# Splitting streamed fp32 weights in place, two chunks ahead, in a two-block transformer kernel

## What is computed

```python
h = x                                                   # first block, 256 tokens
u = rmsnorm(h, g_mix)
qa, ka, va, qb, kb, vb = split(u @ w_in, 6)
h = h + concat(rmsnorm(dilated(qa, ka, va)), rmsnorm(moba(qb, kb, vb))) @ w_out
h = h + memory_cross_attention(rmsnorm(h, g_cross), rmsnorm(mem, g_mem), ...)
h = h + conv_ffn(rmsnorm(h, g_ffn), w_gate, w_up, conv_w, conv_b, w_down)
xl, xc = rmsnorm(h, g_final), ctx                       # second block, 256 + 256 tokens
for l in range(2):
    sh1, sc1, g1, ... = split(silu(c) @ ada_w[l] + ada_b[l], 9)      # the same for c_ctx
    xl = post_norm(xl, 0.5 * g1 * swiglu(modulate(xl, sh1, sc1), ffn1_w_in[l], ffn1_w_out[l]))
    # xc in the same way; then the mixer, the even one (gated linear attention and latent
    # attention) for l = 0, the odd one (neighbourhood attention) for l = 1:
    xl = post_norm(xl, g2 * mixer(modulate(xl, sh2, sc2), modulate(xc, ...)))
    xl = post_norm(xl, 0.5 * g3 * swiglu(modulate(xl, sh3, sc3), ffn2_w_in[l], ffn2_w_out[l]))
    # xc too, but not after the last mixer
```

## Time and profile before

| | |
|---|---|
| median of 3 runs | 2248.92 us (2247.44 to 2249.53) |
| the profiled execution | 2245.71 us, of which its span 2243.9 us |
| granted TensorE clock | 0.998 of full speed |
| PE busy | 2195.9 us, 98% of the span, 13158 matmuls |
| DVE, ACT, POOL busy | 1392.7, 937.4 and 685.3 us |
| DMA | 329.94 MB, 147 GB/s on average |

### The profile page before, as it was taken

The page is one execution under the profiler, slowest core; times in us unless marked ns, Lnnn a source line. Parts: engine busy times, 40 slices in busy tenths (PEclk is TensorE's granted clock), DMA queues, the critical chain, the costliest instruction groups (busy, mean ns, idle before and its releaser), DMA issues. The chain is left out here.

```text
span 2243.9 us, 33497 instructions
## 1 busy us (share of the span) xinstructions
PE 2195.9 (98%) x13158; PEld 1893.8 (84%) x13158; DVE 1392.7 (62%) x2125; ACT 937.4 (42%) x1552; POOL 685.3 (31%) x321
## 2 busy tenths in 40 slices
PE   8999999999999999989999999999999999989999
PEld 8988899998888877757788888788888878879998
DVE  4655454478878577675776675687655484347335
ACT  5664455542222255354522223342222254465443
POOL 3433345422222233221122222412222243213444
PEclk9999999999999999999999999999999999999999
DMA  8446545554554322111244533334544262214553
GB/s 304 153 187 244 188 161 196 174 198 175 191 225 163 107 96 78 66 39 38 104 161 147 189 142 120 106 140 170 196 174 162 88 156 88 76 39 167 169 194 110
DMA packets 79579, 329.94 MB, mean 147 GB/s; under 512 B 19088, under 2 KB 29456, under 8 KB 55872
## 3 DMA queue, kind: packets, MB, share of 16 engines
q1 hardware_dynamic: 79424, 327.81, 41.2%
HBM read 326.70 MB, written 1.08 MB: 146 GB/s over the span
## 5 line engine op out<-in xcount | busy, mean ns | idle before, releaser
L2280 POOL TENSOR_TENSOR WL<-WF,WH 128x1024 fp32r<-128x1024 f32 (+1 forms) x244 | 580.8, 2381 | 1347.8 <-ACT WH L1098 1347.4
L554 PE MATMUL ps<-Hh,WH 128*128 128x256 f32 (+1 forms) x2288 | 593.1, 338 | 3.5 <-ACT Hh L1227 1.5
L558 PE MATMUL ps<-Hh,WL 128*128 128x256 f32 (+1 forms) x2288 | 589.5, 337 | 2.6 <-DVE WL L1624 2.1
L562 PE MATMUL ps<-Hl,WH 128*128 128x256 f32 (+1 forms) x2288 | 588.9, 336 | 0.8 <-DVE Hl L1634 0.8
L1098 ACT CAST WH<-WF 128x1024 fp32r<-128x1024 f32 (+2 forms) x501 | 460.9, 957 | 283.7 <-PE ps L562 265.0
L554 PEld LDWEIGHTS ps<-Hh,WH 128*128 128x128 f32 x2288 | 393.8, 190 | 54.9 <-issue 8.0
L558 PEld LDWEIGHTS ps<-Hh,WL 128*128 128x128 f32 x2288 | 394.8, 190 | 49.3 <-DVE WL L1624 3.8
L562 PEld LDWEIGHTS ps<-Hl,WH 128*128 128x128 f32 x2288 | 395.0, 190 | 46.1 <-DVE Hl L1634 1.0
L1702 DVE CUSTOM_DVE_ANT_0 TMP<-AR 128x1024 f32<-128x1024 f32 x216 | 394.9, 1868 | 17.8 <-DMA AR<-in_ada 16.9
L1624 DVE TENSOR_TENSOR WL<-WF,WH 128x1024 fp32r<-128x1024 f32 (+2 forms) x263 | 313.8, 1194 | 101.7 <-ACT WH L1098 101.1
L558 PE MATMUL ps<-HIDh,WL 128*128 128x512 f32 (+1 forms) x880 | 305.4, 347 | 1.6 <-DVE WL L1624 1.6
(11 more groups left out here) (264 smaller groups left out, 2241.2 us busy)
## 6 DMA issues: line engine op xcount, KB each, us to landing
WF<-in_w SPq DMA_DIRECT2D x170, 1024.0 KB, 4.8
AR<-in_ada SPq DMA_DIRECT2D x120, 512.0 KB, 5.7
WF<-in_w SPq DMA_DIRECT2D x80, 704.0 KB, 4.1
AR<-in_piece SPq DMA_DIRECT2D x12, 1024.0 KB, 7.7
AR<-bias_rows SPq DMA_DIRECT2D x12, 256.0 KB, 7.1
AR<-in_rpb SPq DMA_DIRECT2D x12, 256.0 KB, 6.4
AR<-in_cond SPq DMA_DIRECT2D x2, 1024.0 KB, 7.4
X<-in_x SPq DMA_DIRECT2D x2, 512.0 KB, 4.1
```

The source lines that it names most:

```text
L554: e.matmul(b, h[:, k, col], hi[:, 0:T], start=x == 0, stop=False)
L558: e.matmul(b, l[:, k, col], hi[:, 0:T], start=False, stop=False)
L562: m = e.matmul(b, h[:, k, col], lo[:, 0:T], start=False, stop=x == n - 1)
L2280: e.tensor_tensor(l[:, k0:k1, :], src[:, k0:k1, :], h[:, k0:k1, :].bitcast(F32), ALU.subtract).then_inc(*up("p_lo", ("lo", i, q)))
```

## The change

The staged chunk and the low part now share memory: four buffers, each seen as `WF[i]` (fp32) and as `WL[i]` (F32R), so that DVE and POOL write the low part over the chunk they read. The high part has three buffers. The number of bytes is the same (seven chunks' worth). Chunk i+2 is split at position i everywhere, into slots that chunk i-3 of its own number frees. The hand-written splits in the seams are gone, POOL casts no weights any more except half 1 of chunk 0, and `eout` and `nout` split at all four c. In `pool_mixer_out` the additions of squares at c == 2 now come ahead of the splits. SP waits for the end of chunk i-4 before it loads chunk i, and the modulation step is called for chunk i-2 instead of i-3. Cut to its core:

```diff
-    WF = [sb(f"WF{i}", SLOT)[:, :] for i in range(3)]
-    WH = [None, None]
-    WL = [None, None]
-    for i in range(2):
-        WH[i], WL[i] = sb(f"WH{i}", SLOT, F32R)[:, :], sb(f"WL{i}", SLOT, F32R)[:, :]
+    WF, WL = [], []
+    for i in range(4):
+        with nc.sbuf_tensor(f"WL{i}", [P, SLOT], F32R) as low:
+            pass
+        WL.append(low[:, :])
+        WF.append(sb(f"WF{i}", SLOT)[:, :])
+    WH = [sb(f"WH{i}", SLOT, F32R)[:, :] for i in range(3)]
...
-        return WF[i % 3][:, 0:n].rearrange("p (k c) -> p k c", k=nk(i))
+        return WF[i % 4][:, 0:n].rearrange("p (k c) -> p k c", k=nk(i))
 
     def parts_of(i):
-        n, s = chunk_floats(PLAN[i]), TURN[i] % 2
-        return (WH[s][:, 0:n].rearrange("p (k c) -> p k c", k=nk(i)),
-                WL[s][:, 0:n].rearrange("p (k c) -> p k c", k=nk(i)))
+        n = chunk_floats(PLAN[i])
+        return (WH[i % 3][:, 0:n].rearrange("p (k c) -> p k c", k=nk(i)),
+                WL[i % 4][:, 0:n].rearrange("p (k c) -> p k c", k=nk(i)))
...
-        n = TURN[i]
-        if n + 1 < len(WIDE) and WIDE[n + 1] in SECOND or i in SECOND:
-            return [WIDE[n + 2]]
-        return [WIDE[n + 1]] if n + 1 < len(WIDE) and not (n and WIDE[n - 1] in SECOND) else []
-
-
-
-    SECOND = {CH[name][j] for name, j in (("f0_gu", 1), ("f10_gu", 1), ("e_lr", 0), ("f20_gu", 1),
...
+        return [i + 2] if i + 2 < len(PLAN) else []
+
+    LAST = "f21"
...
-        n = TURN[i]
-        if n < 2:
+        if i < 3:
             return None
-        old = WIDE[n - 2]
+        old = i - 3
...
-        act_half(e, CH["f10_gu"][1], 0)
         act_root(e, "final", S, D, 0)
-        act_half(e, CH["f10_gu"][1], 1)
...
-        i = AFTER[st]
-        if i:
-            act_half(e, i, 0)
...
-            if c < 3:
-                act_splits(e, CH["eout"][c])
+            act_splits(e, CH["eout"][c])
             if c == 2:
-                act_half(e, CH["f20_gu"][0], 0)
                 for k in range(4):
                     act_collect(e, "mix0", k, T2)
-                act_half(e, CH["f20_gu"][0], 1)
...
+        act_split(e, 1)
...
-                if j == 7:
-                    act_half(e, CH["qm"][0], 0)
                 act_square(e, HT[j], X[:, j, lat], ("wsq", j), ("wx", j))
-        act_half(e, CH["qm"][0], 1)
...
+        act_splits(e, CH["vm"][3])
...
-            if k == 3:
-                dve_split(e, AFTER[before], 1)
...
-        if AFTER[st]:
-            dve_split(e, AFTER[st])
...
-        last, [then] = CH[name][3], splits_at(CH[name][3])
         for c in range(4):
-            if c < 2:
-                dve_splits(e, CH[name][c])
-            if c in (1, 2):
-                dve_split(e, last, c - 1)
+            dve_splits(e, CH[name][c])
...
-                if j == 7:
-                    for q in range(2 if T == T2 else 1):
-                        dve_split(e, then, 1 - q)
...
-    def pool_round(e, i):
-
-        src, (h, _) = staged(i), parts_of(i)
-        k0, k1 = halves(i)[1]
-        e.wait_ge(*at(("wf", i)))
-        if slot_freed(i, 1):
-            e.wait_ge(*at(slot_freed(i, 1)))
-        e.tensor_scalar(h[:, k0:k1, :], src[:, k0:k1, :], 1.0, None, ALU.mult).then_inc(*up("p_hi", ("hi", i, 1)))
-
-    def pool_end_norm(e, st):
-        if AFTER[st]:
-            pool_round(e, AFTER[st])
...
-        pool_end_norm(e, st)
...
-        for c in range(3):
-            if c < 2:
-                pool_splits(e, CH[name][c])
+        for c in range(4):
             if c == 2:
-                if T < T2:
-                    pool_split(e, splits_at(CH[name][3])[0], 0)
                 for k in (1, 2, 3):
                     pool_collect(e, st, k, T)
-        pool_end_norm(e, st)
+            pool_splits(e, CH[name][c])
...
-        if i >= 3:
-            old = i - 3
-            for q in range(len(halves(old))):
-                e.wait_ge(*at(("hi", old, q)))
-                e.wait_ge(*at(("lo", old, q)))
+        if i >= 4:
+            e.wait_ge(*at(("end", i - 4)))
         src = bass.AP(a_w.tensor, int(starts[i]), [[n, P], [1, n]])
-        e.dma_start(WF[i % 3][:, 0:n], src).then_inc(*dma(f"wf{i % 3}", ("wf", i)))
+        e.dma_start(WF[i % 4][:, 0:n], src).then_inc(*dma(f"wf{i % 4}", ("wf", i)))
...
-            if i - 3 in MOD_STEP:
-                sp_mod_step(e, *MOD_STEP[i - 3])
+            if i - 2 in MOD_STEP:
+                sp_mod_step(e, *MOD_STEP[i - 2])
```

More of the change, by code:

```diff
@@ L355, in program @@
         CH.setdefault(c[0], []).append(i)
-    WIDE = list(range(len(PLAN)))
-    TURN = {i: n for n, i in enumerate(WIDE)}
     def nk(i):
@@ L367, in staged @@
         n = chunk_floats(PLAN[i])
-        return WF[i % 3][:, 0:n].rearrange("p (k c) -> p k c", k=nk(i))
+        return WF[i % 4][:, 0:n].rearrange("p (k c) -> p k c", k=nk(i))
     def parts_of(i):
-        n, s = chunk_floats(PLAN[i]), TURN[i] % 2
-        return (WH[s][:, 0:n].rearrange("p (k c) -> p k c", k=nk(i)),
-                WL[s][:, 0:n].rearrange("p (k c) -> p k c", k=nk(i)))
+        n = chunk_floats(PLAN[i])
+        return (WH[i % 3][:, 0:n].rearrange("p (k c) -> p k c", k=nk(i)),
+                WL[i % 4][:, 0:n].rearrange("p (k c) -> p k c", k=nk(i)))
     def splits_at(i):
-        n = TURN[i]
-        if n + 1 < len(WIDE) and WIDE[n + 1] in SECOND or i in SECOND:
-            return [WIDE[n + 2]]
-        return [WIDE[n + 1]] if n + 1 < len(WIDE) and not (n and WIDE[n - 1] in SECOND) else []
-    SECOND = {CH[name][j] for name, j in (("f0_gu", 1), ("f10_gu", 1), ("e_lr", 0), ("f20_gu", 1),
-                                          ("f11_gu", 1), ("n_q", 0), ("f21_gu", 1))}
-    AFTER = {"f10": CH["e_lr"][0], "mix0": CH["f20_gu"][1], "f20": CH["f11_gu"][1], "f11": CH["n_q"][0], "mix1": CH["f21_gu"][1],
-             "f21": None}
+        return [i + 2] if i + 2 < len(PLAN) else []
+    LAST = "f21"
     ROUNDED = ("f10", "f20", "f11")
     def slot_freed(i, q):
-        n = TURN[i]
-        if n < 2:
+        if i < 3:
             return None
-        old = WIDE[n - 2]
+        old = i - 3
         same = (nk(old), chunk_floats(PLAN[old])) == (nk(i), chunk_floats(PLAN[i]))
@@ L856, in pe_means @@
         e.matmul(s2[:, 0:T], avg, TMP[6][:, 0:T], start=False, stop=True).then_inc(*up("stat", (st, "m2")))
-        if AFTER[st]:
+        if st != LAST:
             pe_idle(e, st, 4 if T == T2 else 3, ident, cst("gmask")[:, 0:512], ("const2",))
@@ L1531, in act_odd @@
         for c in range(4):
-            if c < 3:
-                act_splits(e, CH["nout"][c])
+            act_splits(e, CH["nout"][c])
             if c == 2:
-                act_half(e, CH["f21_gu"][0], 0)
                 for k in range(4):
                     act_collect(e, "mix1", k, S)
-                act_half(e, CH["f21_gu"][0], 1)
             if c >= 2:
@@ L1548, in act_program @@
                        *([("xsum", 1)] if k == 7 else []))
-        act_half(e, WIDE[0], 0)
+        act_half(e, 0, 0)
         e.wait_ge(*at(("const",)))
@@ L1577, in act_program @@
             act_highs(e, (k, k + 1), {j: HT[j - 4] for j in range(4, 8)}, "yh", "yt")
-            act_half(e, CH["wout"][1], k // 2 - 2)
         for c in range(4):
-            if c:
-                act_splits(e, CH["wout"][c])
+            act_splits(e, CH["wout"][c])
             for j in (2 * c, 2 * c + 1):
-                if j == 7:
-                    act_half(e, CH["qm"][0], 0)
                 act_square(e, HT[j], X[:, j, lat], ("wsq", j), ("wx", j))
-        act_half(e, CH["qm"][0], 1)
         act_root(e, "cross", S, D, 0)
         act_highs(e, range(KT), [HT[8 + k % 6] for k in range(KT)], "ch0", "ct")
+        act_splits(e, CH["vm"][3])
         for t in range(2):
@@ L1598, in act_program @@
                 act_square(e, HT[j], X[:, j, lat], ("osq", j), ("ox", j))
-        act_half(e, CH["f0_gu"][1], 0)
         act_root(e, "ffn", S, D, 0)
[L1601 to L1604, removed]
+        act_highs(e, range(KT), [HT[8 + k % 6] for k in range(KT)], "fh", "ft")
         act_f0(e)
@@ L1827, in dve_f0 @@
                 dve_add(e, n, ("f0", "d", h, n), ("f0", "x", h, n))
-        dve_split(e, CH["f10_gu"][1])
         e.wait_ge(*at(("root", "final")))
@@ L1934, in dve_end_norm @@
         e.wait_ge(*at((st, "mu")))
-        for k in range(2 if AFTER[st] else 4):
+        for k in range(4 if st == LAST else 2):
             dve_centre(e, st, k, T)
@@ L2201, in dve_program @@
             e.tensor_tensor(HT[0], HT[0], HT[1 + (k - 1) % 6], ALU.add).then_inc(*up("d_sum", ("xsum", k)))
-        dve_split(e, WIDE[0])
-        dve_norm(e, "x", "g_mix", [HT[7 + k % 6] for k in range(KT)], "ut", "uh", "ul", WIDE[0])
+        dve_split(e, 0)
+        dve_norm(e, "x", "g_mix", [HT[7 + k % 6] for k in range(KT)], "ut", "uh", "ul", 0)
+        dve_split(e, 1)
         for c in range(2):
@@ L2230, in dve_program @@
                 dve_add(e, j, ("wout", j), ("wx", j))
-        dve_split(e, CH["qm"][0])
```

(10 more changed lines are left out.)

## The result

The changed kernel takes 2255.33 us (median of 7 runs, 2251.51 to 2257.67) against 2247.99 us for the kernel before (7 runs, 2245.85 to 2249.53). The ratio is 1.0036, with a 95% interval of 1.0026 to 1.0045: slower by 7.3 us (6 to 10 by the interval), where 2248.5 was forecast and 2254 was the end of the range. The profiled execution took 2255.93 us (span 2253.8), 10.2 us more than that of before, which was 2.3 us faster than its kernel's median.

A forecast was written before the change was run, and what follows sets the result against it. PE, busy 98% of the 2243.9 us span, was taken as the bound, so only its waits could be won. Terms -9.3 + 0.5 + 1.8 + 2.4 + 4.2 = -0.4 us gave a median of 2248.5, range 2242 to 2254.

The forecast's parts named there:

- The late splits: Fourteen places where PE stood for late weight parts or seam splits; all would go, gaining 9.3 us.
- rival 4: Stalls removed are taken up by PE's next wait; half of 9.3 kept, +4.3 us or 2253.2; chance 0.11.
- In place, and loads later: Low parts written over their input, and chunks loaded when chunk i-4 ends; both taken to cost nothing.
- ACT would wait 0.1 us: ACT's wait for a load at the shortest chunks, down chunks at 256 tokens; harmless until loads exceed 8 us.
- rival 3: Each load over 8 us adds its excess at 32 down chunks, making the kernel slower; chance 0.02.
- The feed-forward seams of the second block stay as they are.: No cost there: PE's fp32 means set the pace, and `SUM` and `SQ` are done a chunk earlier.
- The mixers' ends: POOL's low parts hold up DVE's additions with two SBUF inputs: loss 2.4 us in the even mixer, 4.2 odd.
- Position `e_k0`: Added split there: ACT's two casts go ahead of its two copies, so PE's next chunk starts 1.8 us later.
- 0, if the gates come sooner, to 2.0: Range in us given for the 1.8 us loss at `e_k0`, where ACT's copies follow its gates and casts.
- rival 2: POOL's low parts also hold DVE's four dependent additions per level in the even mixer's attention, 2.0 us each; chance 0.10.
- The odd mixer: Behind its pair, two 1 MB loads start together while ACT has results to copy: 0.5 us lost (0 to 1.5).
- A sign that was given: The prediction counts as wrong if attention, left untouched, moves by more than 2 us.

The follow-up runs named there:

- e8: e6 with DVE's reduction that frees a PSUM bank moved ahead of its low part at gate/up chunk 4 of `f0`; 2238.68 us, ratio to before 0.9961.
- e4: Kernel before with only the changed kernel's memory (low parts in place, later loads), split positions and seams kept; 2247.28 us, ratio to before 0.9994.
- e1: Changed kernel with POOL's low parts held back behind DVE's work on the sums at five seams; 2245.61 us, ratio to before 0.9993.
- e9: Changed kernel with two (even mixer) and five (odd mixer) idle PE matmuls ahead of the wait for `SUM`; 2250.83 us, ratio to before 1.0012.
- e2: Changed kernel with ACT's two copies of `e_k0`'s results ahead of its two casts there; 2261.75 us, ratio to before 1.0065.
- e6: e1 with the mixers' first held low part back ahead of the square additions, and no split at `e_k0`; 2239.52 us, ratio to before 0.9967.
- e7: Changed kernel with four (even mixer) and ten (odd mixer) idle PE matmuls ahead of the wait for `SUM`; 2256.71 us, ratio to before 1.0043.
- e10: e8 with four idle PE matmuls ahead of the wait for POOL's decays in the even mixer's gated attention; 2236.38 us, ratio to before 0.9954.

## Why the prediction was wrong

The losses came to 10.9 us more than the sum gave: 3.8 in the feed-forward seams, 3.1 at and behind `e_k0`, 2.9 in the mixers' ends, 1.1 in the odd mixer.

- **The late splits (-9.3 us).** Right in place: -9.9. That the size fits as well is in part luck, since two errors cancel. In `f0` PE caught up with a PSUM bank that DVE frees behind its low part, and 1.3 us of the lead went there. This is rival 4 in one place, and e8 removes it. At `n_v0` 1.5 us more came: before, PE's clock was at half from 1850 to 1853, behind the wait of 2.07 us in the earlier trace rows, which the count left out.
- **In place, and loads later (0).** The price was right: e4 shows it for the write in place, the changed kernel's waits of PE for the loads. But "ACT would wait 0.1 us" was far too low: it waited 88.5 us in 40 times, and the slack of the splits took that up. Such waits were named as a sign for rival 3; they cost PE nothing, so rival 3 is out all the same.
- **"The feed-forward seams of the second block stay as they are."** This step failed, for 3.8 us. Their sums are not done a chunk earlier, nor complete up to tile 5 or 6 before the last chunk, as the description of the seams says: those of tiles 4 to 6 are added while the last chunk runs (before 1447.30 to 1450.98, the chunk from 1446.30 to 1454), beside a low part of the next pair, and the rule used for the mixers applied to them as well. e1 gives the 3.8 us back. The seam of `f10` has the collision too but lost 0.3 us only: the next chunk there has low parts of half the size, POOL's took 1.64 us from 810.14, and DVE's addition at 810.55 took 1.77 in place of 0.68.
- **The mixers' ends (+2.4, +4.2).** The mechanism was right, down to DVE's 2.8 us and to which operation is hit second. The sum priced the wait and left out what a wait of 2 to 5 us does to PE: 1.7 us each for half clock. With it, 4.1 and 5.9, against 3.9 and 5.6 measured. e9 separates the two parts.
- **Position `e_k0` (+1.8).** PE's wait was there, 1.5 us longer than before's. But "0, if the gates come sooner, to 2.0" bounded only that wait, and the stretch up to `eout0` lost 4.8 us. The step followed the chain on ACT. The one that counts is DVE's gate chain, which stands behind its own low part and is held by POOL's two low parts in a row, as e2 shows. e6, which takes the split out, gives back 3.6 us. The clock has a share: behind 987 us, where only the stretches at 988 and 992 differ, 2.1 of the 4.8 us were lost, the stretch at 855 is new as well, and before's at 938 is missing after. How the 4.8 us divide is not settled. The hits on DVE are rival 2, given 0.10, in the mixer that it named but not on its operations: the four dependent additions of a level took 0.42 us each, and the addition and scans of the decays were held. (Rival 2's 2256.1 for four hits should be 2256.5: 2248.92 - 0.4 + 8.0.)
- **The odd mixer (+0.5).** Behind the pair ACT did wait for a load, 2.2 us at 1858, and PE lost nothing by it: its lag is 4.7 us at 1860 and at 2001. The 1.6 us of that row all come behind it, with the stretches at half clock at 2002 and 2012; e9 had neither and lost nothing there. That 1.6 is near the range of the term is luck.
- **A sign that was given.** The prediction was to be wrong "if attention, which I left untouched, moves by more than 2 us". PE's waits there for DVE (13.1 us in the earlier trace rows) fell to 10.3, and the even mixer's attention lost as said above.

So three things failed: a rule applied in two places where it held in five, a clock taken as constant because the page showed 0.998, and at `e_k0` a chain followed on ACT and not on DVE.

## What to carry to other kernels

Before moving an instruction on POOL, list what DVE does with two SBUF inputs in the same 2.4 us, in every stage and not just in the one whose code changes. In a kernel whose PE is 98% busy, price a new wait of PE of 2 us or more at the wait plus up to 1.7 us, and try to fill those that can't be removed with idle matmuls that fit inside them. When versions differ by a few us, look at the clock in the profiles of several kernels with the same code in a stage before giving its loss to a cause: the even mixer's attention varied by 3 us here. The splits two chunks ahead were worth 7 us here, but only after low parts had been moved at five seams and one position had been taken back (e6).

## What the runs showed of the hardware

- DVE's additions, subtractions and scans from SBUF took up to 2.2 us longer in the places above where a low part of POOL had already started (2.80 against 0.69, 2.88 against 0.68, 3.10 against 0.95 for two). The Trainium skill (SBUF — State Buffer, Who interferes with whom) states this as an exclusive hold for the whole instruction, and these rows agree. The rows before at 1450.02 don't fit as simply: POOL's low part is recorded 0.28 us ahead of DVE's next addition, yet POOL's took 5.57 us instead of 2.4 and DVE lost nothing.
- In the 12 profiled executions PE waited for 2 us or more in 41 places that idle matmuls didn't fill. In 34 of them the granted clock fell to 1.2 GHz in the wait or within 1.6 us of its end, for 3.4 us or twice that. In 7 it didn't, among them 3.57 us in the changed kernel (939) and 3.07 in the kernel before (974). It fell too after waits of 1.1 to 1.9 us, in some executions and not in others, and at 844 to 851 in seven executions with no wait over 0.5 us just ahead. In the two waits on `SUM` and the one at the attention level that idle matmuls filled, it didn't fall (e7, e9, e10). What else decides isn't shown.
- The medians of kernels that differ by a few us can move with the number of such stretches: two in the profiled execution of before, nine after, five in e8's.
